# Hybrid encoder block on one core: the down projection turned round (activations stationary, weights streamed), with a final norm by partitions

## The reference

```python
u = rmsnorm(h, norm_mix_g)
proj = u @ w_in                      # 2048 -> 4928
ret_out, mla_out = retention(proj), latent_attention(proj)      # 8 heads each
h = h + jnp.concatenate([ret_out, mla_out], -1) @ w_o           # 2048 -> 2048
m = rmsnorm(h, norm_mlp_g)
h = h + jnp.square(jax.nn.relu(m @ w_up)) @ w_down              # 2048 -> 8192 -> 2048
return rmsnorm(h[frames], final_norm_g)                         # 256 frames of 2048
```

## Time and profile before

| what | value |
|---|---|
| time, median of 3 runs (lowest, highest) | 1176.4 us (1176.1, 1179.35) |
| time of the profiled execution | 1175.34 us |
| its span, first to last instruction | 1173.5 us |
| mean granted TensorE clock | 0.994 |
| weights moved | 203.84 MB read, 175 GB/s over the span |
| instructions | 18946 |

### The profile page before, as it was taken

One profiled execution on the slowest core, in us unless ns is written; L12 is line 12 of the kernel. 1 busy time (PEld: TensorE's weight loads), 2 busy tenths in 40 slices (PEclk: granted clock), 3 DMA queues, 4 the chain that ended last, 5 costly groups with the idle time before them and its releaser, 6 DMA issues.

```text
span 1173.5 us, 18946 instructions
## 1 busy us (share of the span) xinstructions
PE 1145.9 (98%) x6758; PEld 1003.3 (85%) x6758; DVE 725.6 (62%) x969; ACT 613.2 (52%) x949; POOL 136.6 (12%) x162
## 2 busy tenths in 40 slices
PE   7999999999999999999999999999999999999995
PEld 6888888988888888888888888888888888888884
DVE  6976777676776666666665444445666665444443
ACT  7555455554555555555554444444555555444441
POOL 0011111111122330000000111110000000111111
PEclk9999999999999999999999999999999999999998
DMA  9643424333327555545554555545554555555521
GB/s 357 222 171 118 150 108 170 134 134 134 111 76 279 179 185 197 192 179 181 194 197 179 182 183 208 179 179 188 197 188 179 183 195 192 181 183 184 205 107 71
DMA packets 29980, 206.33 MB, mean 176 GB/s; under 512 B 3456, under 2 KB 3712, under 8 KB 6528
## 3 DMA queue, kind: packets, MB, share of 16 engines
q1 hardware_dynamic: 28512, 199.35, 47.2%
q10 hardware_dynamic: 1440, 6.61, 1.5%
HBM read 203.84 MB, written 2.10 MB: 175 GB/s over the span
## 4 chain that ended last, share of the span: by engine, by line
PE 93%; DVE 3%; ACT 1%; DMA 1%; SPq 1%; issue 0%; DVEq 0%
PE acc L292 84%; PE ps_qn L292 3%; PE ps_qr L292 2%; PE ps_y L292 1%; PE ps_v L292 1%; DMA raw<-w_in 1%; PE ps_x L292 1%; PE ps_kn L292 1%; DVE lo L868 0%; DVE res L868 0%; ACT hi L568 0%; DVE x_sq L868 0%; ACT x_sq L619 0%; SPq L235 0%; DVE hid L1154 0%
## 5 line engine op out<-in xcount | busy, mean ns | idle before, releaser
L868 DVE TENSOR_TENSOR lo<-raw,hi 128x1024 fp32r<-128x1024 f32 (+1 forms) x369 | 451.1, 1223 | 237.4 <-ACT hi L568 233.3
L292 PE MATMUL acc<-xs,hi 128*128 128x512 f32 (+1 forms) x1952 | 588.0, 364 | 0.0
L568 ACT ACTIVATE hi<-raw 128x1024 fp32r<-128x1024 f32 (+1 forms) x369 | 387.3, 1050 | 210.7 <-PE acc L292 206.5
L292 PE MATMUL acc<-xs,lo 128*128 128x256 f32 (+1 forms) x1648 | 456.5, 285 | 9.9 <-DVE xs L885 7.0
L292 PE MATMUL acc<-hid,hi 128*128 128x512 f32 x1280 | 446.9, 396 | 3.2 <-DVE hid L1154 3.2
L292 PEld LDWEIGHTS acc<-xs,hi 128*128 128x128 f32 x1952 | 345.4, 189 | 51.7
L292 PE MATMUL acc<-hid,lo 128*128 128x256 f32 x1280 | 353.1, 282 | 0.0
L292 PEld LDWEIGHTS acc<-xs,lo 128*128 128x128 f32 x1648 | 311.5, 189 | 17.9 <-issue 7.3
L292 PEld LDWEIGHTS acc<-hid,hi 128*128 128x128 f32 x1280 | 238.0, 188 | 55.5 <-DVE hid L1154 4.5
L292 PEld LDWEIGHTS acc<-hid,lo 128*128 128x128 f32 x1280 | 242.2, 189 | 4.2
L568 ACT ACTIVATE half_b<-acc 128x256 f32<-128x256 f32 x132 | 50.9, 386 | 212.7 <-PE acc L292 212.7
(11 more groups left out here) (175 smaller groups left out, 614.1 us busy)
## 6 DMA issues: line engine op xcount, KB each, us to landing
raw<-w_up SPq DMA_DIRECT2D x64, 1024.0 KB, 4.8
raw<-w_down SPq DMA_DIRECT2D x64, 1024.0 KB, 4.8
raw<-w_in SPq DMA_DIRECT2D x37, 1024.0 KB, 4.8
raw<-w_o SPq DMA_DIRECT2D x16, 1024.0 KB, 4.8
side<-w_side ACTq DMA_DIRECT2D x8, 768.0 KB, 6.4
res<-x_frames SPq DMA_DIRECT2D x1, 2048.0 KB, 7.9
x_in<-x_all SPq DMA_DIRECT2D x3, 544.0 KB, 8.4
out<-res SPq DMA_DIRECT2D x2, 640.0 KB, 3.0
```

The source lines that it names most:

```text
L292: return pe.matmul(o, l, m, start=start, stop=stop)
L568: return act.activation(o, i, ACT.Copy)
L868: return dve.tensor_tensor(o, a, b, op)
```

## The change

- In the down projection the hidden activations become the stationary operand (a hi or lo tile of 128 hidden features by 128 frames) and the weights stream past it, 512 output features at a time: for each of 4 groups of 512 output features, each of 2 tiles of 128 frames and each hidden tile, three matmuls of 512 columns (`down_part`). A result lies as frames x features in one bank for each frame tile, in two sets of banks that take turns. The host lays `w_down` out by groups of 512 features, 8 chunks for a group and half.
- The residual stream moves to `h_res`, in the upper part of `hid`, and is loaded earlier. While the output projection runs, PE transposes it tile by tile, 32 transposes in all (`turn`), and ACT copies the result to `res` (`turned_read`), now frames x features.
- After each group DVE adds both banks to `res` (`group_add`). ACT's copies to `half_b`, POOL's and DVE's sums of the down blocks, and POOL's sums of squares go.
- The final norm's sum of squares goes along the free axis: ACT squares with an accumulator for each group and frame tile (`square`). The final gain comes as a 1 MB tile of its own, `gfin`, loaded after `w_o` over constants no longer used, and DVE multiplies with it for each group (`group_gain`), the last group's at the very end. In the last group PE finishes frame tile 0 before frame tile 1. Root and reciprocal are one value for each partition; ACT scales features 0 to 1023, DVE the rest. Three stores in place of four.
- PE's output projection blocks and its down projection, ACT's output projection blocks, and both splits of the down projection are written out without loops.

```diff
-B_HALF = HALF_F + KT
+TILES = FRAMES // P
+GROUP = 512
+GROUPS = D // GROUP
+PER_CHUNK = W // GROUP
+DOWN = HALF_F // PER_CHUNK
...
+        here[0] = hid_at + (2 * KT * TOK + HEADS * FRAMES + 640 + 3 * P) * 4
+        h_res = place("h_res", [KT, FRAMES])
+        assert here[0] <= rest_at
...
+        gfin = consts[:, K_DIST:K_DIST + D]
         ident = consts[:, K_ID:K_ID + P]
...
-            sp.wait_ge(sem["mla_o"], HEADS)
-            sp.wait_ge(sem["gate"], HEADS)
-            sp.wait_ge(sem["gate_exp"], HEADS)
-            sp.wait_ge(sem["ret_v"], 2 * HEADS)
-            sp.dma_start(res[:], x_frames).then_inc(sem["x_back"], 16)
+            sp.wait_ge(sem["mla_s_ps"], HEADS)
+            sp.dma_start(h_res[:], x_frames).then_inc(sem["x_back"], 16)
             with sp.Fori(1, KT // 4) as i:
                     load(w_o[4 * i + j], C_WO + j, 4 * i)
+            for done in ("decay", "mla_s", "rq_ready", "rk_ready", "qr_ready"):
+                sp.wait_ge(sem[done], HEADS)
...
                         load(w_down[4 * i + half * HALF_F + j], C_MLP + half * C_HALF + HALF_F + j, 4 * i)
-            for a, b in zip(STORES, STORES[1:]):
-                on_pool = sum(k < b for k in POOL_SCALED)
-                sp.wait_ge(sem["fin_out"], b - on_pool)
-                sp.wait_ge(sem["fin_pool"], on_pool)
-                sp.dma_start(out[:, a:b, :], res[:, a:b, :]).then_inc(sem["stored"], 16)
-            sp.wait_ge(sem["stored"], 16 * (len(STORES) - 1))
+            sp.wait_ge(sem["fin_act"], 1)
+            sp.wait_ge(sem["fin_dve"], 2)
+            sp.dma_start(out[:, 0, :], res[:, 0, :]).then_inc(sem["stored"], 16)
+            sp.wait_ge(sem["fin_act"], 2)
+            sp.dma_start(out[:, 1, 0:ACT_SCALED], res[:, 1, 0:ACT_SCALED]).then_inc(sem["stored"], 16)
+            sp.wait_ge(sem["fin_dve"], 4)
+            sp.dma_start(out[:, 1, ACT_SCALED:], res[:, 1, ACT_SCALED:]).then_inc(sem["stored"], 16)
+            sp.wait_ge(sem["stored"], 48)
...
             wide(C_WO, C_WO, lambda k: hid_wide(WO_ORDER[k]), lambda k: hid_hi(WO_ORDER[k]), ready=mixed)
-            for j in range(1, 4):
+            def turn(j):
+                pe.wait_ge(sem["acc_read"], C_WO + j + 1)
+                if j % 4 == 0 and j:
+                    pe.wait_ge(sem["ht"], TILES * (j // 4))
+                for t in range(TILES):
+                    m = pe.transpose(turned[t][:, j % 4 * P:j % 4 * P + P], h_res[:, j, t * P:t * P + P], ident)
+                if j % 4 == 3:
+                    m.then_inc(sem["ht_ps"], 1)
+            for j in range(1, KT):
                 wo_block(C_WO + j)
+                turn(j - 1)
...
                 if half == 0:
+                    turn(KT - 1)
                     pe.wait_ge(sem["h_ss"], KT)
...
+                cd = c0 + HALF_F
+                def down_part(g, kk, t, j):
+                    c, k = cd + DOWN * g + kk, PER_CHUNK * kk + j
+                    a = down_acc[g % 2][t][:]
+                    x_h = hid[:, k, META + t * P:META + t * P + P]
+                    x_l = hid[:, k, TOK + META + t * P:TOK + META + t * P + P]
+                    wh = hi[c % 2][:, j * GROUP:(j + 1) * GROUP]
+                    wl = lo[c % 2][:, j * GROUP:(j + 1) * GROUP]
+                    mm(a, x_h, wh, k == 0, False)
+                    mm(a, x_h, wl, False, False)
+                    return mm(a, x_l, wh, False, k == HALF_F - 1)
+                def down_wait(g, kk, j):
+                    c = cd + DOWN * g + kk
+                    if j % 2 == 0:
+                        pe.wait_ge(sem["lo_ready"], 2 * c + j // 2 + 1)
+                    if g == 0:
+                        pe.wait_ge(sem["up_lo"], half * HALF_F + PER_CHUNK * kk + j + 1)
+                def down_chunk(g, kk):
+                    for j in range(PER_CHUNK):
+                        down_wait(g, kk, j)
+                        for t in range(TILES):
+                            m = down_part(g, kk, t, j)
+                        if j % 2 == 1:
+                            m.then_inc(sem["chunk_used"], 1)
+                for g in range(GROUPS):
+                    before = half * GROUPS + g - 1
+                    if before > 0:
+                        pe.wait_ge(sem["dn_h"], TILES * before)
+                    elif before == 0:
+                        pe.wait_ge(sem["ht"], TILES * KT // 4)
+                    last = half == 1 and g == GROUPS - 1
+                    for kk in range(DOWN - 2 if last else DOWN):
+                        down_chunk(g, kk)
+                    if last:
+                        for t in range(TILES):
+                            for kk in range(DOWN - 2, DOWN):
+                                for j in range(PER_CHUNK):
+                                    down_wait(g, kk, j)
+                                    m = down_part(g, kk, t, j)
+                            m.then_inc(sem["dn_ps"], 1)
         @block.scalar
...
                 act.wait_ge(sem["acc_read"], C_WO + j0 + 1 + more)
-                act.activation(sq[:], res[:, j, :], ACT.Square).then_inc(sem["h_sq"], 1)
-                act.activation(xs[:, j, META:TOK], res[:, j, :], ACT.Identity,
+                act.activation(sq[:], h_res[:, j, :], ACT.Square).then_inc(sem["h_sq"], 1)
+                act.activation(xs[:, j, META:TOK], h_res[:, j, :], ACT.Identity,
                                scale=gain(G_MLP + j)).then_inc(sem["m_hi"], 1)
-            with act.Fori(0, KT // 4) as i:
-                for j in range(4):
-                    wo_block(4 * i + j, j, 4 * i)
+            def turned_read(n):
+                act.wait_ge(sem["ht_ps"], n + 1)
+                for t in range(TILES):
+                    copy(res[:, t, n * GROUP:(n + 1) * GROUP], turned[t][:]).then_inc(sem["ht"], 1)
+            for j in range(KT):
+                wo_block(j, j)
+                if j % 4 == 0 and j:
+                    turned_read(j // 4 - 1)
             for half in range(2):
...
                 if half == 1:
-                    act.wait_ge(sem["dn_ss"], KT)
+                    act.wait_ge(sem["dn_h"], TILES * GROUPS)
                 for j in range(4):
                     up(j, j, root=half == 0 and j == 0)
+                    if half == 0 and j == 0:
+                        turned_read(GROUPS - 1)
...
+                cd = c0 + HALF_F
+                def square(g, t):
+                    act.wait_ge(sem["dn_h"], TILES * (GROUPS + g) + t + 1)
+                    if g or t:
+                        act.wait_ge(sem["fin_ss"], TILES * g + t)
+                    act.activation(fin_sq[:], res[:, t, g * GROUP:(g + 1) * GROUP], ACT.Square,
+                                   accum_out=fin_ss[:, t, g:g + 1]).then_inc(sem["fin_ss"], 1)
+                for g in range(GROUPS):
+                    for kk in range(DOWN):
+                        split_hi(cd + DOWN * g + kk + 2, 0)
+                        split_hi(cd + DOWN * g + kk + 2, 1)
+                        if half == 1 and g and kk == 0:
+                            for t in range(TILES):
+                                square(g - 1, t)
+            for t in range(TILES):
+                square(GROUPS - 1, t)
+                act.wait_ge(sem["fin_ss"], TILES * (GROUPS - 1) + t + 1)
+                act.wait_ge(sem["fin_pre"], 3)
+                act.activation(fin_sd[:, t:t + 1], fin_ss[:, t, GROUPS - 1:], ACT.Sqrt, bias=fin_pre[:, t:t + 1],
+                               scale=1.0 / D).then_inc(sem["fin_sd"], 1)
+                act.wait_ge(sem["fin_rstd"], t + 1)
+                act.activation(res[:, t, 0:ACT_SCALED], res[:, t, 0:ACT_SCALED], ACT.Identity,
+                               scale=fin_rstd[:, t:t + 1]).then_inc(sem["fin_act"], 1)
         @block.vector
...
+                cd = c0 + HALF_F
+                def group_add(g, t):
+                    part = res[:, t, g * GROUP:(g + 1) * GROUP]
+                    tt(part, down_acc[g % 2][t][:], part, ALU.add).then_inc(sem["dn_h"], 1)
+                def group_gain(g):
+                    dve.wait_ge(sem["gfin"], 16)
+                    dve.wait_ge(sem["fin_ss"], TILES * (g + 1))
+                    for t in range(TILES):
+                        part = res[:, t, g * GROUP:(g + 1) * GROUP]
+                        tt(part, part, gfin[:, g * GROUP:(g + 1) * GROUP], ALU.mult).then_inc(sem["fin_g"], 1)
+                if half == 0:
+                    dve.wait_ge(sem["ht"], TILES * KT // 4)
+                for g in range(GROUPS):
+                    for kk in range(DOWN):
+                        split_lo(cd + DOWN * g + kk + 2, 0)
+                        split_lo(cd + DOWN * g + kk + 2, 1)
+                        if half == 1 and g and kk == 2:
+                            group_gain(g - 1)
+                    if half == 0 or g < GROUPS - 1:
+                        dve.wait_ge(sem["chunk_used"], 2 * (cd + DOWN * (g + 1)))
+                        for t in range(TILES):
```

(65 more changed lines are left out.)

82 lines of the change are left out of this document (23 added, 59 removed).

## The result

| | before | after |
|---|---|---|
| time, median of 6 runs (lowest, highest) | 1176.33 us (1175.61, 1179.35) | 1168.71 us (1168.02, 1171.83) |
| ratio, 95% interval | | 0.9938 [0.9926, 0.995] |
| span of the profiled execution | 1173.5 us | 1166.9 us |
| instructions | 18946 | 17095 |
| POOL busy | 136.6 us | 76.5 us |

A forecast was written before the change was run, and what follows sets the result against it. PE was taken to bound the kernel except in the 15.1 us tail. The terms -1.6 + 3.5 - 7.6 = -5.7 us against 1175.34 gave 1169.6, or 1170.7 us on the median's footing; range 1164.5 to 1177 us.

The forecast's parts named there:

- Term 1: Down projection on PE: 1536 matmuls of 512 columns at 232.5 ns take 357.1 us, 1.6 us less.
- Term 2: Residual transposes on PE during the output projection: 32 at 0.11 us each, 3.5 us more.
- Term 3: Tail after the last matmul: 7.5 us in place of 15.1, so 7.6 us less.
- (a): Down projection: the splits on ACT and DVE stay and cost nothing under 5.6 us of PE a chunk.
- (b): Down projection: DVE's group adds (11 us), gain products (4 us) and ACT's squares cost nothing under PE.
- (c): ACT's copies of turned banks cost nothing; tightest in the first up projection, with 1.5 us of slack.
- (d): SP and its queue: the earlier 2 MB frames' load and the added 1 MB `gfin` cost nothing.
- (e): Before the output projection PE's wait for the heads stays, as does the low clock after it, 0.83.
- 1: Rival on the transposes: each costs its full 0.27 us, 8.7 in place of 3.5 us, total 1175.9; 12%.
- 2: Rival on the down projection: a 512-column matmul in one piece costs 236.5 ns, total 1176.9 us; 13%.
- 3: Rival on the down projection: the extra over column time is per matmul, 228.5 ns each, total 1164.5 us; 12%.
- 4: Rival: ACT's and DVE's writes hold up PE's down-projection stream; slower from 238.5 ns a matmul, 1184.5 us at 241.5; 8%.

The follow-up runs named there:

- e4: Changed kernel with each 512-column matmul of the second half's down projection cut into two of 256; ratio to the kernel before 0.9955, that stage 180.27 us against 177.71.
- e8: Changed kernel with the last frame tile scaled by ACT in two pieces and stored piecewise, four stores in all; ratio to the kernel before 0.9936, tail 7.07 us.
- e9: Changed kernel with the three down matmuls reordered: lo weights on hi part, hi on hi, hi on lo; ratio to the kernel before 0.9936, down projections 177.49 and 177.71 us.
- e10: Changed kernel with both the matmul order of e5 and the four stores of e8; ratio to the kernel before 0.9919, median 1166.84 us.
- e6: Changed kernel with ACT and DVE writing each split a second time from the second group of the second half's down projection on; ratio to the kernel before 0.9959.
- e7: Changed kernel with the frames' load again waiting for the heads' last events, about 19 us later; ratio to the kernel before 0.9939.
- e2: Changed kernel with every transpose issued twice, 64 in place of 32; ratio to the kernel before 0.9963.
- e5: Changed kernel with the three down matmuls reordered: hi weights on hi part, hi on lo, lo on hi; ratio to the kernel before 0.9927, down projections 176.64 and 176.81 us.

## Why the prediction was right, point by point

- **The bound.** PE bounds all stages behind the heads and the tail is the other lever: right. The 60 us that POOL lost and the 32 blocks' copies and sums show in no stage.
- **Term 1.** Forecast -1.6 us, measured -3.6 (1.8 a half). The sign held, and the size was off by 2 us: I took 232.5 ns for a matmul and it is 231.1 to 231.2. The term that was mis-sized is the middle between single and double; the single distance was the nearer row. Read to the ns, it was 231.8 for the single ones of the earlier trace rows and 233.3 for the double. What brings the gain is only in part shown: fewer matmuls over the same columns are worth at most 1.7 us of the 3.6 by e4. The upper end (236.5 ns from the earlier trace rows) did not come; no run tells what one piece or two makes by itself.
- **Rule and row.** The Trainium skill, "TensorE: Matmul & The Clock Gate", section Back-to-back issue gap, has N/2.4 + 2.5 ns. Its 2.5 ns are near the 3.3 that an extra matmul costs in the pieces of 256; the part by the column is not its 0.417 but 0.445 to 0.449. The trace decides: 231 ns where the rule says 216.
- **Term 2.** Forecast +3.5. A turn is 0.22 us in the trace and 0.44 when doubled: right to 0.1 us. The 3.0 us for leaving float32 were rightly left out. The output projection grew by 3.9 us, of which 15 turns explain 3.3. In the ten profiles whose kernels leave this stage alone it took 98.9 to 99.3 us at a mean granted clock of 0.93 from 340 to 365 us (seven of them; before's is 0.93 too) and 99.9 to 100.2 at 0.86 (e8, e9 and e10). So at a like clock 0.2 to 0.6 us are left over, which no run explains. The same skill's section PE-mode transpose gives 275 ns for one; recorded are 272, paid for are 110.
- **Term 3.** Forecast -7.6, measured -7.6, and the exact hit is luck: two errors of 0.4 to 0.5 us cancel. The chain to the last product took 3.2 us in place of 3.6 (DVE's two products 1.14 in place of 1.38, as the one with one value for each partition has 0.48 for 512 columns and not 0.69; the rest is in the handovers), and stores and issue together took 4.4 in place of 3.9.
- **Under cover.** (a) held, with a thinner cover in the last group than I had said (e6). (b) held: in neither down projection of the changed kernel are two starts of PE over 240 ns apart. (c) held: the second block's z ended at 460.17 and PE began the fourth at 462.19, 2.0 us of slack where I had 1.5. (d) held as to the frames' load (e7). (e) held: 0.83 from 353 to 363 us again.
- **The sum.** -5.7 forecast for the profiled execution, -6.6 measured: -2.0 from term 1, +0.7 from the output and the up projection beyond the 3.5 of the turns, and +0.4 from the stage before, where PE's work is the same. The medians are 7.6 us apart since before's profiled execution lay 1 us under its median and after's did not. That the total came within 2 us owes something to errors of both signs.
- **The rivals.** 1 is out by e2, 2 by the distances (231.1 ns, not 236.5), 3 by e4 as a cost that every matmul has, 4 by e6's trace, with DVE and ACT busy 1.7 times as long.

## What to carry to other kernels

Where PE bounds, count columns first: turning a product round left them as they were and gave 3.6 us of 359, half of it for reasons that stay open, while most of the gain came from what the turned layout does to the tail, where a norm over partitions (ones matmul, root and reciprocal of 256 values, products on the full tile) becomes one value for each partition, and where one tile's chain can run under the other's matmuls. A slower run is not yet evidence for the theory that foretold it: look where the idle time lies.

## What the runs showed of the hardware that was not expected

- Two float32r matmuls in a row with the same stationary tile are not cheaper than with two different ones; the streams that have them are dearer by a mean of 3.3 ns for each such place (e5, e9: 177.49 against 176.64 us for 768 matmuls with 256 such places). Each matmul has its own weight load in the records either way.
- A float32r matmul of 512 columns costs 231 ns at a granted clock of 1.00 (2.4 GHz, 213.3 ns for its columns), and cut in two it costs 3.3 ns more (e4): nearly all of the excess goes with the columns, 0.445 to 0.449 ns each in place of 0.417. Where these 7 to 8% go is open; more writes of ACT and DVE do not change it (e6).
- The work before the output projection took between 344.4 and 348.4 us in thirteen profiles, and the output projection itself 98.9 to 100.2 us in the ten that leave it alone; an unedited up or down projection behind it repeated to 0.07 us, most to 0.02. The scatter of this kernel's time comes from before 450 us, and the granted clock goes with a part of it (e8, e9, e10).
